# Up products of a ConvFFN: the two column halves taken in turn, pass by pass, under the same weights

## What is computed

```python
def conv_ffn(h, conv0, w_up, conv_w, w_down):
    up = h @ w_up                       # 1024 -> 2 * 2816: gate | val
    gate, val = up[..., :D_FF], up[..., D_FF:]
    gate, conv_new = causal_dwconv(gate, conv0, conv_w)     # three taps along the tokens
    return (jax.nn.silu(gate) * val) @ w_down, conv_new
```

## Time and profile before

| | |
|---|---|
| median of three runs | 2079.63 us (2076.84 to 2080.99) |
| the profiled execution's own time | 2076.17 us |
| its span, first to last instruction | 2074.4 us |
| mean granted TensorE clock | 0.972 of full speed |
| TensorE matmuls busy | 1902.2 us, 92% of the span, 14814 matmuls |
| TensorE weight loads busy | 1773.5 us, 14814 loads |
| VectorE / ScalarE / GpSimd busy | 49% / 32% / 43% |
| DMA | 97 GB/s over the span |

### The profile page before, as it was taken

One profiled execution on the slowest core, in us unless ns is written; L12 is line 12 of the kernel. 1 busy time (PEld: TensorE's weight loads), 2 busy tenths in 40 slices (PEclk: granted clock), 3 DMA queues, 4 the chain that ended last, 5 costly groups with the idle time before them and its releaser, 6 DMA issues.

```text
span 2074.4 us, 38392 instructions
## 1 busy us (share of the span) xinstructions
PE 1902.2 (92%) x14814; PEld 1773.5 (85%) x14814; DVE 1019.8 (49%) x1627; ACT 659.7 (32%) x1101; POOL 886.4 (43%) x753
## 2 busy tenths in 40 slices
PE   6999968878798999999998999888988999999998
PEld 4999968777796999999997899655557999999997
DVE  3888545556445552452446523555553353353352
ACT  3553323343331432221222221344443332222221
POOL 3445533144053654564567232000005754465465
PEclk9999989999998999999999999999999999999999
DMA  4222310000055422322312231687781423222221
GB/s 124 61 71 71 81 27 21 1 0 0 2 141 162 118 81 82 92 81 71 89 54 80 86 119 54 214 299 251 273 294 42 126 81 87 86 81 82 81 65 56
DMA packets 250353, 201.63 MB, mean 97 GB/s; under 512 B 7541, under 2 KB 230007, under 8 KB 250017
## 3 DMA queue, kind: packets, MB, share of 16 engines
q1 hardware_dynamic: 241092, 170.48, 27.6%
q10 hardware_dynamic: 9164, 29.80, 4.0%
HBM read 187.72 MB, written 12.53 MB: 97 GB/s over the span
## 4 chain that ended last, share of the span: by engine, by line
PE 76%; DVE 9%; ACT 4%; issue 4%; DMA 2%; ACTq 2%; POOL 1%; SPq 0%; DVEq 0%; POOLq 0%
PE PS L662 73%; DVE f L1293 4%; PE PS L665 4%; ACT f L1844 2%; DVE f L1396 1%; ACT f L1847 1%; DVE f L1290 1%; POOL f L2285 1%; ACTq L2194 1%; ACT L1844 1%; ACTq L2192 1%; DVE r L1293 1%; DMA f<-in_cache_k 1%; DMA f<-in_a_w_in 1%; DMA f<-in_f_conv_w 0%
## 5 line engine op out<-in xcount | busy, mean ns | idle before, releaser
L662 PE MATMUL PS<-r,r 128*128 128x288 f32 (+2 forms) x9888 | 1318.6, 295 | 14.8 <-issue 7.1
L662 PEld LDWEIGHTS PS<-r,r 128*128 128x128 f32 x9888 | 1302.9, 189 | 19.1 <-issue 9.3
L1293 DVE TENSOR_TENSOR f<-PS,f 128x512 f32<-128x512 f32 (+10 forms) x463 | 227.5, 517 | 550.0 <-PE PS L662 524.2
L2438 POOL TENSOR_TENSOR r<-f,r 128x1024 fp32r<-128x1024 f32 x128 | 311.9, 2439 | 309.8 <-ACT r L1847 309.3
L1847 ACT ACTIVATE r<-f 128x1024 fp32r<-128x1024 f32 (+5 forms) x263 | 259.8, 998 | 484.9 <-PE PS L662 391.4
L662 PE MATMUL PS<-f,f 128*32 128x256 f32 (+14 forms) x2124 | 240.5, 376 | 45.3 <-POOL f L2285 12.9
L1847 ACT ACTIVATE f<-PS 128x512 f32<-128x512 f32 (+3 forms) x230 | 124.7, 560 | 371.3 <-PE PS L665 195.8
L665 PE MATMUL PS<-f,f 128*128 128x128 f32 (+5 forms) x1226 | 177.0, 288 | 70.6 <-DVE f L1293 27.6
L2285 POOL TENSOR_TENSOR f<-f,f 128x512 f32<-128x512 f32 (+1 forms) x155 | 143.9, 947 | 227.3 <-DVE f L1293 152.1
L662 PEld LDWEIGHTS PS<-f,f 128*32 128x32 f32 (+4 forms) x2124 | 146.4, 145 | 106.5 <-issue 65.3
L665 PEld LDWEIGHTS PS<-f,f 128*128 128x128 f32 (+5 forms) x1226 | 139.9, 149 | 106.4 <-issue 50.5
(11 more groups left out here) (74 smaller groups left out, 707.0 us busy)
## 6 DMA issues: line engine op xcount, KB each, us to landing
f<-in_f_w_up SPq DMA_DIRECT2D x88, 512.0 KB, 3.9
f<-in_cache_k SPq DMA_DIRECT2D x64, 512.0 KB, 4.9
f<-in_cache_v ACTq DMA_DIRECT2D x56, 512.0 KB, 6.2
f<-in_a_w_in SPq DMA_DIRECT2D x32, 512.0 KB, 4.3
f<-in_f_w_down SPq DMA_DIRECT2D x32, 512.0 KB, 3.9
f<-in_a_w_out SPq DMA_DIRECT2D x16, 512.0 KB, 4.7
f<-in_w_kv SPq DMA_DIRECT2D x8, 1024.0 KB, 5.5
out<-f SPq DMA_DIRECT2D x13, 512.0 KB, 4.7
```

The lines of the kernel that those rows point to most:

```text
L662: return nc.tensor.matmul(out, lhsT, rhs, start=start, stop=stop)
L1293: return V.tensor_tensor(out, a, b, op)
L2438: G_.tensor_tensor(upW.lo2[n], upW.raw2[n], upW.hi_f[n], ALU.subtract).then_inc(w_lo, 1)
```

## The change

The loop over the column halves goes from the outside of the product to its inside. For each block k, the three pairs of weights and stream are taken in the order of before, and each is multiplied with half 0 and then half 1. So a product still has 48 passes, on the same operands and into the same two banks, but the passes go to bank 2n and bank 2n + 1 in turn, and of the 48 the same weights serve four passes in a row (hi with xh and xl, both halves) and then two (lo with xh, both halves). The first pass into each bank has the start flag and the last one the stop flag. The eight `xl_ready` waits of a layer's first product now stand six passes apart, not three.

```diff
-                            for h in range(2):
-                                c = slice(h * HALF, (h + 1) * HALF)
-                                for k in range(KB):
-                                    if p == 0 and n == 0 and h == 0:
-                                        pe.wait_ge(xl_ready, X_F[l] + k + 1)
-                                    last = mm3(PS[:, 2 * n + h, 0:HALF], upW.hi[n][:, k, :], upW.lo[n][:, k, :],
-                                               xh[:, k, c], xl[:, k, c], k == 0, k == KB - 1)
+                            for k in range(KB):
+                                if p == 0 and n == 0:
+                                    pe.wait_ge(xl_ready, X_F[l] + k + 1)
+                                for w, x in ((upW.hi[n], xh), (upW.hi[n], xl), (upW.lo[n], xh)):
+                                    for h in range(2):
+                                        last = mm(PS[:, 2 * n + h, 0:HALF], w[:, k, :], x[:, k, h * HALF:(h + 1) * HALF],
+                                                  k == 0 and w is upW.hi[n] and x is xh, k == KB - 1 and w is upW.lo[n])
                             last.then_inc(ft_done, 1)
```

## The result

The changed kernel is slower. Seven runs of each have medians of 2088.16 us (2080.99 to 2093.4) and 2080.16 us before (2074.08 to 2082.58); the ratio is 1.0035, with a 95% interval of 1.0021 to 1.0049. At 2080 us this is 7.3 us, between 4.4 and 10.2. The forecast was 2079.6 us and no change, in a range of 2073 to 2087 us.

What follows compares the result with a forecast made beforehand. TensorE alone was taken to bound the ConvFFNs, by passes times the distance of their starts. All terms summed to 0, so no change (chance 0.80) at the runs' median scale, 2079.6 us, range 2073 to 2087 us.

Steps and rivals of the forecast that it cites:

- What bounds the stage: ConvFFN up products: time is 4224 passes times the 132.0 ns between starts, 557.6 us; other engines wait for TensorE.
- It is not the load's length, and not a change of weights: Up passes: the 12 ns over 120 ns come from neither, since loads can follow at 117 ns and repeats gain nothing.
- free loads: Up passes: repeated weights become free, four of six passes drop to 120 ns, 33.8 us faster, 2046 us; chance 0.03.
- The rows on 256-column passes: Profile rows: 256-column passes with the same 128 x 128 loads go at 117 ns, read as distance following the streamed columns.
- Changes of bank cost zero: Up products: 48 bank changes per product instead of two, each under 5 ns, bounds -21 to +21 us, taken as zero.
- The rival that carried most of the slower side, 0.07: All 4224 up passes: each bank switch waits for something to close; 2.5 ns gives +10.6 us, 2090 us; chance 0.07.
- The rival of the falling clock: Up passes fall to 240 ns each, 108 ns dearer; all of them would be +456 us, 2536 us; chance 0.02.
- The pattern within a run: Up passes: alternating halves cost the mean of 130.9 and 133.5 ns, so no change; outermost bounds -21 and +34 us.
- the near bounds: Up passes: all at the first half's 130.9 ns, -4.6 us, or all at the second half's 133.5 ns, +6.3 us.
- unsettled pattern towards the dear half: Up passes: all take the second half's 133.5 ns, giving 2085.9 us; chance 0.03.
- Both go with the half, and the new order leaves both with the pass: Up passes: a second-half pass is some 2.6 ns dearer, by column start or bank; the new order keeps both.
- Signals, waits, other engines: Up products: later `xl_ready` waits, bank readers and other engines' work stay under cover of TensorE; change 0.

Runs made afterwards that it cites:

- the sweep: Kernel before plus 45 groups of 48 passes at chosen stream and weight starts, behind the last down product; all between 130.0 and 133.3 ns per pass.
- the lower places: All tiles from `O_SM` on moved 48 bytes down, in both orders; against the kernel before, old order 1.0027, new order 0.9991.
- the order by block: Changed kernel with three passes on half 0, then three on half 1 for each block; 131.1 ns per pass in layer 0, 132.2 in layer 1.

## Why the prediction was wrong

*What bounds the stage* was right: the time is 4224 passes times the distance of their starts, and the bound of 1.0 ns per pass for a difference that can be told was the right measure. The distance grew by 1.3.

*It is not the load's length, and not a change of weights*: right. The loads stayed at 187 to 189 ns, and the order with one repeat in six costs the same 102.39 us as the one with four. That free loads were a rival at 0.03 was fair. But "it is not the load" went too far: where the loads read helps to set what a pass costs, as the sweep shows with only the weights moved. The rows on 256-column passes showed that loads can follow each other faster, not that they are without effect.

*Changes of bank cost zero*: right, 130.7 ns with a change at every pass. The rival that carried most of the slower side, 0.07, had the right sign by a mechanism that is not there. The rival of the falling clock did not come either: the stretch with a change at every pass has no gap and a granted clock of 1.00. What the Trainium skill reports in "TensorE: Matmul & The Clock Gate", section "A second HAM failure mode: psum-queue depth-cycling", goes with short idle times between groups; here there were none.

*"The pattern within a run: I take the mean of the two halves, since it is what runs of both add up to now"*: this is the step that failed. It put the order of the halves at 0; the runs showed 133.3 ns for halves in turn where the mean is 132.0, 5.5 us over 4224 passes. That runs of 24 add up was true, but says nothing on a sequence in which no run exists. The long and short distances in the earlier trace rows, which repeat over two passes though all passes of that run are alike, were the sign that a pass has no price of its own: it depends on what went ahead of it. From there nothing on record made the mean likelier than the near bounds, all passes at the cheap price or all at the dear one, and in the sweep none of the eight pairs with the weights at 48 came out at its mean. Nor is the dear bound a rule: at the lower places the new order ran at 130.0 ns in two of three phases, and with the weights moved at 132.1. That it cost what the dear half costs belongs to the places of this kernel. The rival "unsettled pattern towards the dear half" had the place and the size, 4224 x 1.5 = 6.3 us and 2085.9 us, against 5.5 us by the trace and 7.3 us (4.4 to 10.2) by the runs; it had a chance of 0.03, against 0.80 for the mean. The explanation tried for it, that the cheap pattern takes more than a few passes on one half to settle, is not borne out: three passes and three in turn ran at 131.1 and 132.2 ns, not at 133.

*"Both go with the half, and the new order leaves both with the pass"*: the first part was settled as the columns' place and not the bank; the second was the same mistake, since a place has a price only together with its neighbours.

*Signals, waits, other engines*: right, no gap in the stretches, and the other engines busy as before. That the down products keep their times held to 0.1 us per stretch; why they became 0.2 ns per pass dearer was not followed. *The range*: its top, 2087.0 us, was the near bound plus little; the median came 1.2 us above, with 1.6 us of the profiled execution from lower-clock passes that vary by themselves.

What stays open is how stream and weights meet. The runs show that the price is a matter of their places, that it lies between 130.0 and 133.3 ns for 288 columns, and that one sequence can hold two rates. They do not show whether the two reads contend, or for what. Nor do they show what picks one of the two rates: the lower kernel in the new order has 133.3 ns in each layer's first phase and 130.0 in the others, and the order by block differs from layer to layer.

## What to carry to other kernels

Where matmuls follow each other without a gap, measure the distance of their starts against the columns that stream; what is left over can depend on where stream and weights lie in memory and in which order they are read, by 1 to 2% here, and then a reordering that changes no work is a change of that price. Do not add up prices of passes that were measured in runs of their own kind: if equal passes show unequal distances, the price belongs to the sequence, and a new sequence has to be measured. A sweep of the starts in a spare stretch of the kernel costs one run, but only the kernel decides: at the weights' new place the sweep's numbers held to 0.3 ns in all up phases but one, and at the lower places the sweep had 133.1 ns where most phases of the kernel ran at 130.0.

## What was not expected of the hardware

- In a stream without a gap, a pass of 288 fp32r columns takes 130.0 to 133.3 ns at the 2.4 GHz level, by where the columns and the weights start, where 288 columns are 120 ns; at 1.2 GHz it takes 240 ns and nothing is left over.
- 133.3 ns is a ceiling over all places tried: 13 of 45 groups are at it, as is the changed kernel.
- Two starts in turn do not cost the mean of the two: 131.7 and 130.0 ns alone became 133.3 in turn.
- Moving the weights by 80 bytes, with no instruction changed, made the kernel 0.27% faster; moving the tiles from `O_SM` on down by 48 bytes made it 0.27% slower and turned the sign of this change around.
- The same instructions on the same addresses ran at 131.1 ns in one layer and 132.2 ns in the other; with other tile places, at 133.3 ns in the first phase of a layer and 130.0 ns in the next two.
